# A row buffer for each half token tile in the rotation of query and key rows on GpSimd

## The chip, the cores and the metric

The kernel runs on one core of one Trainium2 chip. The metric is the device time of one execution in microseconds (us), as the median of several. Five engines work side by side and each has its own instruction queue: TensorE (PE; its weight loads are listed as PEld), VectorE (DVE), ScalarE (ACT), GpSimd (POOL) and SyncE (SP). Order between engines is kept by semaphores alone: one instruction increments a counter, another waits for it to reach a value. Transfers between HBM (the memory outside the core) and SBUF (the memory in it) run on 16 DMA engines. They are issued from the queue of SP, ACT or POOL, and each increments its semaphore by 16 once its data has landed.

## The reference

The kernel computes one layer of an encoder for 1280 tokens (1024 of one request group and 256 of another) of width 1024. Cut to what matters here:

```python
h = rmsnorm(x, norm_mix)
proj = h @ w_in                     # GLA q/k/v/gate, decay codes, GQA q/k/v, two branch gates
o_a = gla_branch(...)               # gated linear attention, forward and backward scans
o_b = gqa_branch(aq, ak, av, ...)   # 8 query heads, 2 key heads of 128
merged = sigmoid(z_a) * (o_a @ w_o_gla) + sigmoid(z_b) * (o_b @ w_o_att)
x = x + merged @ w_out
x = x + expert_choice_ffn(rmsnorm(x, norm_ffn))   # 16 experts

# within gqa_branch: the part that GpSimd prepares
qh = apply_rope(rmsnorm(qh, q_norm), cos, sin) * HD ** -0.5
kh = apply_rope(rmsnorm(kh, k_norm), cos, sin)

def apply_rope(x, cos, sin):        # pairs of neighbouring elements
    x0, x1 = x[..., 0::2], x[..., 1::2]
    return interleave(x0 * cos - x1 * sin, x0 * sin + x1 * cos)
```

## The kernel before

The program is a row of phases: `project`, `gla`, `mix`, `keys`, `attention`, `mix`, `finish_mixer`, `choose`, `experts`. Each phase is a block with a program for every engine. At its end all engines meet at a barrier (the engines report to a semaphore called gather, on which GpSimd waits, and wait themselves for one called release); a small block on GpSimd clears the phase's semaphores (`Phase.clear`, L95 to L103); then the engines meet again and jump to the next phase. Nothing of a phase starts before the last engine has left the one before.

The change lies in `project`. Tokens are in ten tiles of 128 (NT = 10). After the norm and the transposes of the token tiles, the 5,000-odd columns of `w_in` that this phase needs are taken in units of 512: seven units (NB) with the tokens in the partitions, stored in `proj_t`; two (NA) with the channels in the partitions, stored in `proj_c`; at last the 48 columns of the decay codes, which stay in SBUF. For each unit ACT issues the load of its 2 MB of weights, rounds them to a high part (`hi`, L297), DVE subtracts to get the low part (`lo`, L355), PE multiplies in three passes (L108 to L110 and L121), ACT copies each finished bank to a stage (L302) and SP stores it (L191). The last work of ACT in the phase is the copy of the decay codes (L332).

The first three units hold the attention's queries (1024 columns), keys (256) and values (256). Once their stores have landed (`stored`, 3 x 10 tiles), GpSimd turns the ten heads of each token tile, five heads (HH) at a time, which is half a token tile: 128 partitions x 640 columns, 320 KB. That is `rotate(n, h)`, L224 to L261, for n = 0 to 9 and h = 0, 1:

- it issues the read of the half from `proj_t` into `gamma` (L230), a tile that held the norm's gains earlier; for h = 0 also the reads of the tile's cosines and sines (L233); then it waits for what it issued (L235, L236);
- it squares (L237), sums over each head in seven halving adds (L240), copies the five sums into `ss` (L243), multiplies with the norm's gains into `scaled` (L247), and writes the two outputs of the rotation back over the row (L253 to L256, twice);
- it issues the write of the row back to `proj_t` (L259) and waits until it has landed (L260).

There is one row buffer and one semaphore each for reads and writes. `ph.settle` is an increment of a semaphore that nobody waits for. Of GpSimd's results nothing is used before the `keys` phase, two phases later.

Of the kernel before, what the change touches and what calls it, by code (L numbers as in the profile page):

```python
# [16 lines left out]
P = 128  # L17
# [3 lines left out]
NT, NTS = T // P, TS // P  # L21
# [5 lines left out]
AH, KVH, HD = 8, 2, 128  # L27
# [19 lines left out]
CR = 8  # L47
# [79 lines left out]
def pairs(t, e):  # L127

    return t.rearrange("... (d e) -> ... d e", e=2)[..., e]


def project(nc, x, w_cols, norm_mix, qk_norms, cos, sin, cst, act_hl, proj_t, proj_c, codes, ss):
# [3 lines left out]
    with ExitStack() as ctx:  # L136
        ph = Phase(nc, ctx, "pj")
        RC = 3 * RANK
        gamma = ph.sb("gamma", [P, D])
# [15 lines left out]
        stored = ph.stored("stored", 2)  # L155

        HH = HEADS // 2
        heads = gamma[:, 0:HH * HD].rearrange("p (h d) -> p h d", d=HD)
        scaled, first, second = ph.sb("h_scaled", [P, HH, HD]), ph.sb("h_first", [P, HH, HD // 2]), ph.sb("h_second", [P, HH, HD // 2])
        tab, gains = ph.sb("tables", [P, 2, HD // 2]), ph.sb("qk_gains", [P, 2, HD])  # L160
        gains_in, tab_in, h_in, h_back = (ph.landed(n) for n in ("gains_in", "tab_in", "h_in", "h_back"))
        h_step = ph.done("h_step")
        WIDTHS = [HD >> i for i in range(1, HD.bit_length())]
        HSTEPS = 10 + len(WIDTHS)
        x_d = x.rearrange("(n p) d -> p n d", p=P)
        w_d = w_cols.rearrange("(k p) c -> p k c", p=P)
        t_d = proj_t.rearrange("(n p) c -> p n c", p=P)
# [17 lines left out]
        with nc.Block() as block:  # L185

            @block.sync
            def _(sp):
                def store(q, s, dst, width):
                    sp.wait_ge(p_out, CR + q + 1)  # L190
                    sp.dma_start(dst, stage[:, s, 0:width]).then_inc(stored[s], 16)  # L191

                ph.start(sp)

                def load_x(n, s, i):

                    sp.wait_ge(x_ready, CR + n - 1)
                    sp.dma_start(xt[:, s], x_d[:, bass.ds(n, 1)].rearrange("p n d -> p (n d)")).then_inc(x_in[s], 16)

                tiles(sp, load_x, lambda: sp.dma_start(raw[:, 0], w_d[:, :, 0:UW]).then_inc(w_in[0], 16))  # L200
                sp.wait_ge(h_lo, CR + NT)
                sp.dma_start(raw[:, 1], w_d[:, :, UW:2 * UW]).then_inc(w_in[1], 16)
                with sp.Fori(0, NB) as n:
                    for t in range(NT):
                        store(n * NT + t, t % 2, t_d[:, t, bass.ds(n * UW, UW)], UW)
                with sp.Fori(0, NA) as n:
                    for q in range(3 * MU):
                        a, b = TOK3[q % 3]
                        store(tok_n + n * (3 * MU) + q, q % 2, proj_c[bass.ds(n * UW + q // 3 * P, P), a:b], b - a)
                for s in range(2):  # L210
                    sp.wait_ge(stored[s], ST + 16 * (tok_n + chan_n) // 2)

            @block.gpsimd
            def _(pool):
                pool.dma_start(gamma[:], norm_mix.to_broadcast([P, D])).then_inc(gamma_in, 16)
                pool.dma_start(rraw[:], w_d[:, :, (NA + NB) * UW:(NA + NB) * UW + RC]).then_inc(r_in, 16)
                pool.wait_ge(h_lo, CR + NT)
                for j, g in enumerate(qk_norms):
                    pool.dma_start(gains[:, j], g.to_broadcast([P, HD])).then_inc(gains_in, 16)
                pool.wait_ge(gains_in, 32)  # L220
                for s in range(2):
                    pool.wait_ge(stored[s], ST + 16 * G_V * NT // 2)

                def rotate(n, h):  # L224

                    c = 2 * n + h
                    b = CR + HSTEPS * c
                    rows = t_d[:, bass.ds(n, 1), h * HH * HD:(h + 1) * HH * HD].rearrange("p n c -> p (n c)")
                    flat = gamma[:, 0:HH * HD]
                    pool.dma_start(flat, rows).then_inc(h_in, 16)  # L230
                    if h == 0:
                        for j, src in enumerate((cos, sin)):
                            pool.dma_start(tab[:, j], src.rearrange("(n p) d -> p n d", p=P)[:, bass.ds(n, 1)].rearrange("p n d -> p (n d)")  # L233
                                           ).then_inc(tab_in, 16)
                        pool.wait_ge(tab_in, 32 * n + 32)  # L235
                    pool.wait_ge(h_in, 16 * c + 16)  # L236
                    pool.tensor_tensor(scaled[:], heads, heads, ALU.mult).then_inc(h_step, 1)  # L237
                    pool.wait_ge(h_step, b + 1)
                    for i, w in enumerate(WIDTHS):
                        pool.tensor_tensor(scaled[:, :, 0:w], scaled[:, :, 0:w], scaled[:, :, w:2 * w], ALU.add).then_inc(h_step, 1)  # L240
                        pool.wait_ge(h_step, b + 2 + i)
                    ph.settle(pool)
                    pool.tensor_copy(ss[:, bass.ds(n, 1), h * HH:(h + 1) * HH].rearrange("p n h -> p (n h)"), scaled[:, :, 0]).then_inc(h_step, 1)  # L243
                    b = b + len(WIDTHS)
                    pool.wait_ge(h_step, b + 2)
                    for sl, g in ((slice(0, 3), 0), (slice(3, HH), h)):
                        pool.tensor_tensor(scaled[:, sl], heads[:, sl],  # L247
                                           gains[:, g:g + 1].broadcast_to([P, sl.stop - sl.start, HD]), ALU.mult).then_inc(h_step, 1)
                    pool.wait_ge(h_step, b + 4)
                    cs, sn = (tab[:, j:j + 1].broadcast_to([P, HH, HD // 2]) for j in range(2))  # L250
                    for e, op in ((0, ALU.subtract), (1, ALU.add)):

                        pool.tensor_tensor(first[:], pairs(scaled[:], e), cs, ALU.mult).then_inc(h_step, 1)  # L253
                        pool.tensor_tensor(second[:], pairs(scaled[:], 1 - e), sn, ALU.mult).then_inc(h_step, 1)
                        pool.wait_ge(h_step, b + 6 + 3 * e)
                        pool.tensor_tensor(pairs(heads, e), first[:], second[:], op).then_inc(h_step, 1)  # L256
                        pool.wait_ge(h_step, b + 7 + 3 * e)
                    ph.settle(pool)
                    pool.dma_start(rows, flat).then_inc(h_back, 16)  # L259
                    pool.wait_ge(h_back, 16 * c + 16)  # L260
                    ph.settle(pool)  # L261

                with pool.Fori(0, NT) as n:
                    for h in range(2):
                        rotate(n, h)

            @block.scalar
            def _(act):
# [1637 lines left out]
def program(nc, dram):  # L1906

    with ExitStack() as ctx:
# [26 lines left out]
        with ExitStack() as mixer:  # L1935
            act_hl = mixer.enter_context(nc.sbuf_tensor("act_hl", [P, 2, KC, T], F32R))
            ss = mixer.enter_context(nc.sbuf_tensor("head_squares", [P, NT, HEADS], F32))
            with ExitStack() as scan:
                codes = scan.enter_context(nc.sbuf_tensor("codes", [3 * RANK, T], F32))
                project(nc, dram["x"], dram["w_cols"], dram["norm_mix"], (dram["q_norm"], dram["k_norm"]), dram["cos"], dram["sin"],  # L1940
                        cst, act_hl, proj_t, proj_c, codes, ss)
                gla(nc, proj_t, proj_c, z_c, o_t, dram["w_z"], (dram["w_gk_f"], dram["w_gk_b"]), (dram["b_gk_f"], dram["b_gk_b"]),
                    dram["gla_norm"], dram["masks"], codes, cst, act_hl)
            mix(nc, "mg", act_hl, dram["w_o_gla"], z_c[0:D], gla_g, source=o_t)
            with ExitStack() as kvs:
                kT = kvs.enter_context(nc.sbuf_tensor("kT", [P, 2, KVH, T], F32R))
                vv = kvs.enter_context(nc.sbuf_tensor("vv", [P, 2, NT, KVH * HD], F32R))
                inv = kvs.enter_context(nc.sbuf_tensor("head_inverses", [P, NT, HEADS], F32))
                keys(nc, proj_t, ss, inv, cst, kT, vv)
                attention(nc, proj_t, inv, cst, kT, vv, act_hl)  # L1950
            mix(nc, "ma", act_hl, dram["w_o_att"], z_c[D:2 * D], merged, add=gla_g)
# [55 lines left out]
```

## Time and profile before

| | before |
|---|---|
| median of 3 runs | 3467.0 us (3466.13 to 3467.72) |
| the profiled execution, whole | 3462.08 us |
| its span, first to last instruction | 3460.5 us |
| PE busy in the span | 3064.7 us (89%) |
| DVE busy | 1703.2 us (49%) |
| ACT busy | 1516.4 us (44%) |
| POOL busy | 555.5 us (16%) |
| mean granted clock of TensorE | 0.94 |

The numbers of the profile come from one execution, which here was 4.9 us shorter than the median of the three timed runs. Times in rows are microseconds from the start of the span, durations in ns or us as the view says. The page draws the span in 40 slices of 86.5 us. "Idle before" is time in which an engine stood still just ahead of an instruction, and the name behind the arrow is what ended it; "issue" there means that the profile shows nothing that it waited for.

### The profile page before, as it was taken

Reading aid. Unit: us, or ns where it says so; the run is one execution under the profiler, and the core shown is the slowest. Engines: PE = TensorE matmul, PEld = TensorE weight load, DVE = VectorE, ACT = ScalarE, POOL = GpSimd, SP = SyncE. Lnnn points to the kernel's source line nnn. Section 1 sums busy time; section 2 is a strip of 40 time slices with the busy share of each in tenths; the row PEclk is TensorE's granted clock in tenths of the full one; section 3 lists DMA queues with packets and bytes.
Section 4 is the critical chain, followed back from the end, with each engine's and each line's share of the span. In section 5 each row is a group of like instructions: output and inputs, shape, how many; then the busy total and the mean of one; then the engine's idle time right before and its main releaser. Section 6 shows DMA issues by size and latency. Waiting matters only on the chain. (4 is left out here: it accounts for less than half of the span.)

```text
span 3460.5 us, 51737 instructions
## 1 busy us (share of the span) xinstructions
PE 3064.7 (89%) x19370; PEld 2410.2 (70%) x19370; DVE 1703.2 (49%) x1710; ACT 1516.4 (44%) x1630; POOL 555.5 (16%) x726
## 2 busy tenths in 40 slices
PE   4999996298888769997788399999999999999998
PEld 4888884176667558986667277777777777777776
DVE  4010000144434228994232666766767667666675
ACT  3111110134534216663044265656655656556554
POOL 0016666301211000000100101011111111111100
PEclk7999998599899889999999699999999999999999
DMA  4233321222222430003443478888888878888784
GB/s 153 73 106 119 112 79 60 81 83 93 73 83 68 164 110 25 18 13 113 152 150 115 157 280 285 296 291 281 297 282 284 300 278 289 291 277 284 280 284 164
DMA packets 196331, 600.82 MB, mean 174 GB/s; under 512 B 15184, under 2 KB 45536, under 8 KB 196256
## 3 DMA queue, kind: packets, MB, share of 16 engines
q1 hardware_dynamic: 167056, 509.08, 41.0%
q0 software_dynamic: 21920, 76.03, 7.5%
q10 hardware_dynamic: 7280, 14.68, 1.3%
q8 instruction: 50, 0.82, 0.1%
q14 instruction: 25, 0.20, 0.0%
HBM read 522.33 MB, written 77.33 MB: 173 GB/s over the span
## 5 line engine op out<-in xcount | busy, mean ns | idle before, releaser
L1755 DVE TENSOR_TENSOR ex_w_lo<-ex_w_raw,ex_w_hi 128x2048 fp32r<-128x2048 f32 x384 | 880.0, 2292 | 450.4 <-ACT ex_w_hi L1706 450.3
L1706 ACT ACTIVATE ex_w_hi<-ex_w_raw 128x2048 fp32r<-128x2048 f32 x384 | 735.7, 1916 | 522.0 <-PE ex_ps_s L1842 467.4
L1842 PE MATMUL ex_ps_s<-ex_w_hi,ex_xS 128*128 128x512 f32 x2048 | 578.2, 395 | 0.0
L1842 PEld LDWEIGHTS ex_ps_s<-ex_w_hi,ex_xS 128*128 128x128 f32 x2048 | 375.9, 188 | 99.4 <-issue 26.3
L1842 PE MATMUL ex_ps_s<-ex_w_lo,ex_xS 128*128 128x512 f32 x1024 | 316.4, 390 | 0.0
L1842 PE MATMUL ex_ps_s<-ex_w_hi,ex_hidS 128*128 128x512 f32 x1024 | 307.9, 403 | 0.0
L1853 PE MATMUL ex_ps_p<-ex_w_raw,ex_xP 128*32 128x256 f32 x4096 | 235.5, 382 | 0.0
L1692 POOL DMA_INDIRECT y<-ex_ye_s,ex_rows_y x16 | 43.6, 2724 | 1145.8 <-DVE ex_ye_s L1798 1145.8
L108 PE MATMUL pj_ps_tok<-pj_w_hi,act_hl 128*128 128x512 f32 x560 | 219.1, 391 | 2.7 <-DVE act_hl L350 2.7
L1842 PEld LDWEIGHTS ex_ps_s<-ex_w_lo,ex_xS 128*128 128x128 f32 x1024 | 192.2, 188 | 41.4
L109 PE MATMUL pj_ps_tok<-pj_w_lo,act_hl 128*128 128x512 f32 x560 | 218.8, 391 | 0.0
L110 PE MATMUL pj_ps_tok<-pj_w_hi,act_hl 128*128 128x512 f32 x560 | 218.8, 391 | 0.0
L355 DVE TENSOR_TENSOR pj_w_lo<-pj_w_raw,pj_w_hi 128x4096 fp32r<-128x4096 f32 x9 | 39.8, 4425 | 358.6 <-ACT pj_w_hi L297 358.6
L1842 PEld LDWEIGHTS ex_ps_s<-ex_w_hi,ex_hidS 128*128 128x128 f32 x1024 | 182.8, 188 | 46.7 <-issue 13.2
L1853 PEld LDWEIGHTS ex_ps_p<-ex_w_raw,ex_xP 128*32 128x32 f32 x4096 | 126.8, 110 | 100.3 <-issue 23.9
L302 ACT ACTIVATE pj_stage<-pj_ps_tok 128x512 f32<-128x512 f32 x70 | 41.9, 599 | 308.5 <-PE pj_ps_tok L110 308.5
L108 PE MATMUL gl_z_ps<-act_hl,gl_z_w_hi 128*128 128x512 f32 (+1 forms) x384 | 156.7, 408 | 3.9 <-ACT gl_z_stage L1035 1.9
L1842 PE MATMUL ex_ps_s<-ex_w_lo,ex_hidS 128*128 128x512 f32 x512 | 159.5, 393 | 0.0
L109 PE MATMUL gl_z_ps<-act_hl,gl_z_w_hi 128*128 128x512 f32 (+1 forms) x384 | 141.9, 370 | 0.0
L110 PE MATMUL gl_z_ps<-act_hl,gl_z_w_lo 128*128 128x512 f32 (+1 forms) x384 | 141.7, 369 | 0.0
L108 PEld LDWEIGHTS pj_ps_tok<-pj_w_hi,act_hl 128*128 128x128 f32 x560 | 105.8, 189 | 25.4 <-issue 3.1
L109 PEld LDWEIGHTS pj_ps_tok<-pj_w_lo,act_hl 128*128 128x128 f32 x560 | 105.8, 189 | 22.0
(268 smaller groups left out, 5134.3 us busy)
## 6 DMA issues: line engine op xcount, KB each, us to landing
ex_w_raw<-w_e_gate SPq DMA_DIRECT2D x128, 1024.0 KB, 11.8
ex_w_raw<-w_e_up SPq DMA_DIRECT2D x128, 1024.0 KB, 11.8
ex_w_raw<-w_e_down SPq DMA_DIRECT2D x128, 1024.0 KB, 8.7
proj_t<-pj_stage SPq DMA_DIRECT2D x70, 256.0 KB, 2.0
pj_w_raw<-w_cols ACTq DMA_DIRECT2D x7, 2048.0 KB, 8.6
gl_z_w_raw<-w_z SPq DMA_DIRECT2D x16, 512.0 KB, 3.6
gate_logits<-gl_z_stage SPq DMA_DIRECT2D x32, 256.0 KB, 2.2
pj_gamma<-proj_t POOLq DMA_DIRECT2D x20, 320.0 KB, 3.3
```

Of the source, the lines that this page charges most:

```text
L108: pe.matmul(out, a[0], b[0], start=first, stop=False)
L109: pe.matmul(out, a[0], b[1], start=False, stop=False)
L110: return pe.matmul(out, a[1], b[0], start=False, stop=last)
L302: act.activation(stage[:, s, 0:width], src, ACT.Copy).then_inc(p_out, 1)
L355: dve.tensor_tensor(wlo[:, s], raw[:, s], whi[:, s].bitcast(F32), ALU.subtract).then_inc(w_lo, 1)
L1692: pool.indirect_dma_start(dst, bass.IndirectOffsetOnAxis(ap=rows_y[j][:, 0:1], axis=0), src[:], None, compute_op=ALU.add).then_inc(scatter ...
L1706: act.activation(whl[0][:, j % NHL], raw[:, j % NRAW], ACT.Copy).then_inc(w_hi, 1)
L1755: dve.tensor_tensor(whl[1][:, j % NHL], raw[:, j % NRAW], whl[0][:, j % NHL].bitcast(F32), ALU.subtract).then_inc(w_lo, 1)
L1842: mm = pe.matmul(ps_s[:, s, c:c + 512], x(part, k), whl[w][:, j % NHL, kk, c:c + 512], start=k == 0 and part + w == 0, stop=k == 2 * PU - ...
L1853: mm = pe.matmul(ps_p[CP * c:CP * c + CP, f % 2, 0:QW], x(k, c), raw[:, j % NRAW, k % 2, QW * c:QW * c + QW], start=k == 0, stop=k == 2 * ...
```

## The change

There are now two row buffers: `row_buf[0]` is the old place in `gamma`, `row_buf[1]` a new tile `h_rows` of 128 x 640, one for each half. Reads and writes have a semaphore for each half (`h_in`, `h_back`). `rotate(n, h, follow)` no longer issues its own read. It waits for its row, does the same arithmetic, and between the multiplication with the gains and the rotation proper it calls `follow()`. For h = 0 that is `next_half`: wait until the write of the second half of the tile before has landed, issue the read of this tile's second half, and wait for the tables. For h = 1 it is `next_tile`: wait until the write of this tile's first half has landed, and issue the read of the next tile's first half. The next tile's tables are read after the second half is done. The write back is issued at the end of a half, and nothing waits for it there. The first and the last tile stand outside the loop, and the two waits for the last writes stand behind it.

```diff
-        heads = gamma[:, 0:HH * HD].rearrange("p (h d) -> p h d", d=HD)
+        row_buf = [gamma[:, 0:HH * HD], ph.sb("h_rows", [P, HH * HD])[:]]
...
-                    pool.dma_start(flat, rows).then_inc(h_in, 16)
-                    if h == 0:
-                        for j, src in enumerate((cos, sin)):
...
-                        pool.wait_ge(tab_in, 32 * n + 32)
-                    pool.wait_ge(h_in, 16 * c + 16)
+                def load_half(n, h):
+                    pool.dma_start(row_buf[h], half_rows(n, h)).then_inc(h_in[h], 16)
...
+                def rotate(n, h, follow):
+
+                    b = CR + HSTEPS * (2 * n + h)
+                    heads = row_buf[h].rearrange("p (h d) -> p h d", d=HD)
+                    pool.wait_ge(h_in[h], 16 * n + 16)
                     pool.tensor_tensor(scaled[:], heads, heads, ALU.mult).then_inc(h_step, 1)
...
+                    follow()
                     pool.wait_ge(h_step, b + 4)
...
-                    pool.dma_start(rows, flat).then_inc(h_back, 16)
-                    pool.wait_ge(h_back, 16 * c + 16)
-                    ph.settle(pool)
-
-                with pool.Fori(0, NT) as n:
-                    for h in range(2):
-                        rotate(n, h)
+                    pool.dma_start(half_rows(n, h), row_buf[h]).then_inc(h_back[h], 16)
+
+                def both(n, begin, last):
+
+                    def next_half():
+                        if not begin:
+                            pool.wait_ge(h_back[1], 16 * n)
+                            ph.settle(pool)
+                        load_half(n, 1)
+                        pool.wait_ge(tab_in, 32 * n + 32)
+                        ph.settle(pool)
+
+                    def next_tile():
+                        if not last:
+                            pool.wait_ge(h_back[0], 16 * n + 16)
+                            ph.settle(pool)
+                            load_half(n + 1, 0)
+
+                    rotate(n, 0, next_half)
+                    rotate(n, 1, next_tile)
+                    if not last:
+                        load_tables(n + 1)
+
+                load_half(0, 0)
+                load_tables(0)
+                both(0, True, False)
+                with pool.Fori(1, NT - 1) as n:
+                    both(n, False, False)
+                both(NT - 1, False, True)
+                for h in range(2):
+                    pool.wait_ge(h_back[h], 16 * NT)
```

In GpSimd's queue, inside the loop, the border between the first and the second half of a tile stood like this before (`pj_gamma` is the row buffer; DMA `proj_t<-pj_gamma` is the write back, `pj_gamma<-proj_t` the read; the names in brackets are the semaphores waited for; ISA and REGISTER_ALU are bookkeeping):

```order
L256 TENSOR_TENSOR pj_gamma<-pj_h_first,pj_h_second 128x320 [waits pj_h_step]
L257 REGISTER_ALU
L259 DMA proj_t<-pj_gamma 128x640 [waits pj_h_step]
L230 ISA [waits pj_h_back0]
L230 DMA pj_gamma<-proj_t 128x640
L236 ISA
L237 TENSOR_TENSOR pj_h_scaled<-pj_gamma 128x640 [waits pj_h_in0]
```

and stands like this now, at the same border:

```order
L260 TENSOR_TENSOR pj_gamma<-pj_h_first,pj_h_second 128x320 [waits pj_h_step]
L261 REGISTER_ALU
L263 REGISTER_ALU [waits pj_h_step]
L263 DMA proj_t<-pj_gamma 128x640
L240 TENSOR_TENSOR pj_h_scaled<-pj_h_rows 128x640 [waits pj_h_in1]
```

The wait for the write and the issue of the read have gone from between the two halves; what is left there is the wait for the read alone.

In the middle of a first half stood before, in the same queue:

```order
L247 TENSOR_TENSOR pj_h_scaled<-pj_gamma,pj_qk_gains 128x384 [waits pj_h_step]
L247 TENSOR_TENSOR pj_h_scaled<-pj_gamma,pj_qk_gains 128x256
L249 REGISTER_ALU
L253 TENSOR_TENSOR pj_h_first<-pj_h_scaled,pj_tables 128x320 [waits pj_h_step]
```

and now:

```order
L250 TENSOR_TENSOR pj_h_scaled<-pj_gamma,pj_qk_gains 128x384 [waits pj_h_step]
L250 TENSOR_TENSOR pj_h_scaled<-pj_gamma,pj_qk_gains 128x256
L228 ISA [waits pj_h_back1]
L228 DMA pj_h_rows<-proj_t 128x640
L272 ISA
L253 REGISTER_ALU [waits pj_tab_in0]
L257 TENSOR_TENSOR pj_h_first<-pj_h_scaled,pj_tables 128x320 [waits pj_h_step]
```

The read of the other half and the two waits have come in between the gains and the rotation. On the other engines the same instructions stand in the same order as before; only their line numbers differ.

## Rows read from the trace of the kernel before

**Rows 1.** The page's 40 slices: busy tenths of PE, POOL; granted clock.

```profile
PE   4999996298888769997788399999999999999998
...
POOL 0016666301211000000100101011111111111100
PEclk7999998599899889999999699999999999999999
```

**Rows 2.** The view by windows: stretch, its length, each engine's busy time (count), clock.

```profile
236.60:410.00 173.40, 173.40 (x766) 143.63 (x765) 14.57 (x4) 29.73 (x35) 109.98 (x160) 1.00 0.35 119
410.00:578.00 168.00, 164.91 (x811) 135.06 (x809) 4.43 (x1) 19.48 (x32) 102.88 (x163) 0.99 0.23 77
578.00:656.00 78.00, 0.15 (x2) 0.00 (x0) 0.00 (x0) 1.23 (x1) 48.60 (x78) 0.52 0.11 35
```

**Rows 3.** Timeline of the phase border: last work of ACT and POOL, first of `gla`.

```profile
578.19 1.23 ACT L332 ACTIVATE codes<-pj_ps_chan 48x1280 f32<-48x1280 f32 x1 [15.76 <-PE pj_ps_chan L110]
...
652.40 0.57 POOL L259 DMA_DIRECT2D proj_t<-pj_gamma  x1 [0.71 <-POOL pj_gamma L256]
661.70 1.23 DVE L1212 MEMSET gl_starts<- 128x1408 bf16 x1 [206.21 <-PEq L95]
...
668.37 9.33 PE L1238 MATMUL gl_ring<-codes,gl_w_gate 16*128 16x512 f32 x12 [90.21 <-DMA gl_bias<-b_gk_b]
```

**Rows 4.** Timeline of POOL over one token tile of the loop, from its first read.

```profile
616.16 0.55 POOL L230 DMA_DIRECT2D pj_gamma<-proj_t  x1 [2.95 <-issue]
616.75 0.53 POOL L233 DMA_DIRECT2D pj_tables<-cos  x1
617.28 0.53 POOL L233 DMA_DIRECT2D pj_tables<-sin  x1
620.27 1.24 POOL L237 TENSOR_TENSOR pj_h_scaled<-pj_gamma 128x640 f32<-128x640 f32 x1 [2.46 <-DMA pj_tables<-sin]
...
626.96 0.87 POOL L253 TENSOR_TENSOR pj_h_first<-pj_h_scaled,pj_tables 128x320 f32<-128x320 f32 x1
...
633.14 0.58 POOL L259 DMA_DIRECT2D proj_t<-pj_gamma  x1 [0.81 <-POOL pj_gamma L256]
636.35 0.55 POOL L230 DMA_DIRECT2D pj_gamma<-proj_t  x1 [2.63 <-DMA proj_t<-pj_gamma]
639.64 1.25 POOL L237 TENSOR_TENSOR pj_h_scaled<-pj_gamma 128x640 f32<-128x640 f32 x1 [2.74 <-DMA pj_gamma<-proj_t]
```

**Rows 5.** Groups of POOL's instructions by line, 236 to 656 us; idle before, its releasers.

```profile
L237 POOL TENSOR_TENSOR pj_h_scaled<-pj_gamma 128x640 f32<-128x640 f32 x20 | 24.9, 1246 | 56.1 <-DMA pj_gamma<-proj_t 28.5 <-DMA pj_tables<-sin 27.6
L230 POOL DMA_DIRECT2D pj_gamma<-proj_t x20 | 11.0, 550 | 231.3 <-DMA proj_t<-pj_stage 172.4 <-DMA proj_t<-pj_gamma 32.0 <-issue 26.9
```

**Rows 6.** Two slow transfers: the waits on the row's write, then the tables.

```profile
347.17 0.55 POOL L230 DMA_DIRECT2D pj_gamma<-proj_t  x1 [6.24 <-DMA proj_t<-pj_gamma]
...
540.61 1.24 POOL L237 TENSOR_TENSOR pj_h_scaled<-pj_gamma 128x640 f32<-128x640 f32 x1 [4.59 <-DMA pj_tables<-sin]
```

**Rows 7.** Timeline of DVE, 236 to 455 us: all its work there.

```profile
287.88 4.42 DVE L355 TENSOR_TENSOR pj_w_lo<-pj_w_raw,pj_w_hi 128x4096 fp32r<-128x4096 f32 x1 [49.98 <-ACT pj_w_hi L297]
342.27 4.42 DVE L355 TENSOR_TENSOR pj_w_lo<-pj_w_raw,pj_w_hi 128x4096 fp32r<-128x4096 f32 x1 [49.97 <-ACT pj_w_hi L297]
396.68 4.42 DVE L355 TENSOR_TENSOR pj_w_lo<-pj_w_raw,pj_w_hi 128x4096 fp32r<-128x4096 f32 x1 [49.98 <-ACT pj_w_hi L297]
451.07 4.43 DVE L355 TENSOR_TENSOR pj_w_lo<-pj_w_raw,pj_w_hi 128x4096 fp32r<-128x4096 f32 x1 [49.97 <-ACT pj_w_hi L297]
```

**Rows 8.** Timeline of POOL: the gains' multiplication, beside DVE's work and alone.

```profile
286.93 5.97 POOL L247 TENSOR_TENSOR pj_h_scaled<-pj_gamma,pj_qk_gains 128x384 f32<-128x384 f32 x2
...
310.86 1.71 POOL L247 TENSOR_TENSOR pj_h_scaled<-pj_gamma,pj_qk_gains 128x384 f32<-128x384 f32 x2
...
395.74 5.96 POOL L247 TENSOR_TENSOR pj_h_scaled<-pj_gamma,pj_qk_gains 128x384 f32<-128x384 f32 x2
```

**Rows 9.** The line L355: count, durations in ns (least/median/most).

```profile
L355 DVE TENSOR_TENSOR pj_w_lo<-pj_w_raw,pj_w_hi x9: 4424/4425/4427, 52.6 to 451.1; 128x4096 fp32r<-128x4096 f32 x9
```

**Rows 10.** Timeline at two other phase borders, into `attention` and into `choose`.

```profile
1287.74 2.83 DVE L457 TENSOR_TENSOR kT<-ky_turned,kT 128x2560 fp32r<-128x2560 f32 x1 [1.06 <-ACT kT L442]
...
1292.03 0.53 POOL L539 DMA_DIRECT2D at_q_in<-proj_t  x1 [51.33 <-SPq L83]
...
1904.45 0.27 ACT L1421 ACTIVATE affT<-fm_ps_a 16x128 f32<-16x128 f32 x1 [0.94 <-PE fm_ps_a L1499]
1905.79 0.48 DVE L1558 MEMSET tk_aff<- 96x512 f32 x1 [1.81 <-PEq L95]
```

More of the change, by code:

```diff
@@ L157, in project @@
         HH = HEADS // 2
-        heads = gamma[:, 0:HH * HD].rearrange("p (h d) -> p h d", d=HD)
+        row_buf = [gamma[:, 0:HH * HD], ph.sb("h_rows", [P, HH * HD])[:]]
         scaled, first, second = ph.sb("h_scaled", [P, HH, HD]), ph.sb("h_first", [P, HH, HD // 2]), ph.sb("h_second", [P, HH, HD // 2])
         tab, gains = ph.sb("tables", [P, 2, HD // 2]), ph.sb("qk_gains", [P, 2, HD])
-        gains_in, tab_in, h_in, h_back = (ph.landed(n) for n in ("gains_in", "tab_in", "h_in", "h_back"))
+        gains_in, tab_in, h_in, h_back = ph.landed("gains_in"), ph.landed("tab_in"), ph.landed("h_in", 2), ph.landed("h_back", 2)
         h_step = ph.done("h_step")
@@ L222, in _, with half_rows, load_tables @@
                     pool.wait_ge(stored[s], ST + 16 * G_V * NT // 2)
[L224 to L229, printed above, removed]
-                    pool.dma_start(flat, rows).then_inc(h_in, 16)
-                    if h == 0:
-                        for j, src in enumerate((cos, sin)):
-                            pool.dma_start(tab[:, j], src.rearrange("(n p) d -> p n d", p=P)[:, bass.ds(n, 1)].rearrange("p n d -> p (n d)")
-                                           ).then_inc(tab_in, 16)
-                        pool.wait_ge(tab_in, 32 * n + 32)
-                    pool.wait_ge(h_in, 16 * c + 16)
+                def half_rows(n, h):
+                    return t_d[:, bass.ds(n, 1), h * HH * HD:(h + 1) * HH * HD].rearrange("p n c -> p (n c)")
+                def load_half(n, h):
+                    pool.dma_start(row_buf[h], half_rows(n, h)).then_inc(h_in[h], 16)
+                def load_tables(n):
+                    for j, src in enumerate((cos, sin)):
+                        pool.dma_start(tab[:, j], src.rearrange("(n p) d -> p n d", p=P)[:, bass.ds(n, 1)].rearrange("p n d -> p (n d)")
+                                       ).then_inc(tab_in, 16)
+                def rotate(n, h, follow):
+                    b = CR + HSTEPS * (2 * n + h)
+                    heads = row_buf[h].rearrange("p (h d) -> p h d", d=HD)
+                    pool.wait_ge(h_in[h], 16 * n + 16)
                     pool.tensor_tensor(scaled[:], heads, heads, ALU.mult).then_inc(h_step, 1)
```

## The prediction

> **What bounds the kernel now.** I read the page's slices first. PE is at nine tenths almost everywhere except in a few holes, and one hole is the eighth slice (606 to 692 us): PE 2, clock 5, while POOL shows 3 after four slices of 6 [rows 1]. The view by windows narrows it down. From 236.6 to 578 us PE is busy for 338.3 of 341.4 us, and POOL works beside it. From 578 to 656 us PE is busy for 0.15 us, DVE for nothing, ACT for 1.23 us, and POOL alone works, for 48.60 us of 78 [rows 2]. The timeline says why: ACT's last work of the phase ends at 578.19 + 1.23 = 579.42 us, POOL issues its last write at 652.40 us, and the first work of `gla` starts on DVE at 661.70 us; PE had been idle for 90.21 us when it began again [rows 3]. All engines must have left the phase before the next one starts, so from 579.42 us on the rotation on POOL is the critical path, and nothing covers it. That is the only place where this change can gain, and it can gain no more than the gap: the end is then set by PE and ACT.
>
> Next I asked what POOL's 78 us are made of. One token tile (two halves) takes from 616.16 us to the next read, some 39.8 us. Its arithmetic is 620.27 to 633.14 us for the first half, 12.9 us with its step to the write, and about the same for the second. Between them it stands still four times: 2.46 us for the tables and the row, 2.63 us for the first write to land, 2.74 us for the second row, 2.95 us for the second write (listed as "issue", at the loop's turn) [rows 4]. Over all twenty halves the groups give 56.1 us for reads, and 32.0 + 26.9 us for writes, 115.0 us in all; the 172.4 us in the same row is the wait for the projection's first units and stays [rows 5].
>
> **The change part by part.**
>
> *The waits between halves.* A write is now waited for in the middle of the following half, a read at the start of the half after its issue. The middle of a half is 626.96 - 620.27 = 6.7 us behind its start [rows 4], the slowest write seen was waited for 6.24 us behind its issue, the slowest row or table read 4.59 us [rows 6], so each write has 6.7 us or more before somebody asks for it, and each read has the rest of its half, another 6.2 us, and the write's issue. I take both waits as gone. What stays is the first read (from 3.29 us issue to start, [rows 4]), the last write (2.6 to 2.95 us), and the turn of the loop, 0.3 us by the difference of 2.95 and 2.63, nine times. So 115.0 - 3.3 - 2.6 - 2.9 = about 106 us leave POOL's chain.
>
> *The DMA issues.* POOL still issues twenty reads, twenty writes and twenty table reads at 0.53 to 0.58 us each [rows 4]. The reads stood between halves and stand now in their middle; the count is the same and nobody but POOL waits behind them. Cost: zero, against an upper bound of 0.55 us a half, 11 us in all, if an issue in the middle holds up more than it did at the border.
>
> *Collisions with DVE.* Four times in this stretch DVE splits weights for 4.42 us [rows 7]. At 287.88 and 396.68 us POOL was in the multiplication with the gains, and the pair took 5.97 and 5.96 us in place of 1.71 us [rows 8]: 4.26 us of stall each, just under DVE's whole 4.42 us. At 342.27 and 451.07 us POOL stood in a wait for a DMA, and the stall hid there. With POOL almost never idle all four will count: two more, 8.5 us added. The Trainium skill ("GPSIMD Engine Reference", Key points) says that GpSimd shares its SBUF interfaces with VectorE and contends with DVE instructions that have two SBUF inputs. The rule speaks against this change, since denser POOL work meets more of DVE's, and the trace agrees with it; by the rule as by the rows POOL is held for at most DVE's 4 x 4.42 = 17.7 us. DVE pays nothing: its nine splits lie between 4424 and 4427 ns [rows 9], with POOL in the middle of an operation or not.
>
> *POOL's new end.* Before, POOL left at 652.40 + 0.57 + 2.6 to 2.95 = 655.6 to 655.9 us. Now 655.7 - 106 + 8.5 = 558 us; with the 11 us above, 569 us. ACT's last work ends at 579.42 us. So POOL leaves the path with 21 us to spare (10 in the worse case), and the phase ends with ACT. From there on a faster POOL is worth nothing: of the 98 us that it gains, some 21 are lost as slack.
>
> *PE's stretch.* It stays: PE was busy for 173.40 of 173.40 us while POOL worked for 109.98 us beside it [rows 2], and its order is unchanged.
>
> *The barrier.* This is the one term that the trace does not show directly. Before, from POOL's leaving (655.7) to the first work of `gla` (661.70, [rows 3]) it took 6.0 us. At two borders where another engine than POOL came last it took 1905.79 - 1904.72 = 1.07 us (behind ACT, as here in future) and 1292.03 - 1290.57 = 1.46 us (behind DVE) [rows 10]. So `gla` begins between 580.5 and 585.4 us. I take the nearest kind of border, one with ACT last, near the short end: 580.9 us, since POOL will have come out of its loop long before. The extra 4.6 us I can't explain from the rows; they may belong to POOL's exit from the loop or to this border as such.
>
> *Sum.* 661.70 - 580.9 = 80.8 us less, or 76.3 us with the long barrier. All phases behind it begin with the same barrier and the same loads and are carried forward as they are. Of TensorE: before 661 us it was granted half clock (0.52 over the gap, [rows 2]), and after some 9 us of idle I expect the same start at half clock, so no further gain. The profiled execution would take 3462.1 - 80.8 = 3381.3 us; it stood 4.9 us below the median of the runs, so the median becomes 3467.0 - 80.8 = 3386.2 us.
>
> **The rivals.**
>
> *A: the long barrier stays.* For it: the 6.0 us were measured at this very border, and the release that DVE saw last was PE's, not POOL's [rows 3]. Against: the two borders of [rows 10]. Time: 3467.0 - 76.3 = 3390.7 us.
>
> *B: POOL stays the last engine.* The mechanism: the reads are not hidden, because POOL does not go on while its own transfer is prepared and under way, and only the waits for writes fall (32.0 + 26.9 = 58.9 us, less 2.6 and 2.9 that stay: 53 us) while the two extra stalls come on top (8.5 us). POOL then leaves at 655.7 - 53 + 8.5 = 611 us, the gain is 45 us and the time 3422 us. Against: in [rows 4] the issue of a table read follows 0.04 us after the one before it, while the row's transfer is under way. In a milder form (each half some 1.1 us longer than I think) POOL ends level with ACT, and only beyond that it costs.
>
> *C: slower than before.* The mechanism: POOL's denser traffic holds up DVE's splits and with them PE. The place is the start of each unit (every 54.4 us, [rows 7]). DVE has some 50 us of idle before each split [rows 7], so each would have to grow from 4.4 to over 54 us before PE waits at all, and over the stretch PE would have to lose more than 80.8 us, a quarter of its 341 us, for the kernel to be slower. At a loss of 90 us the time would be 3476 us. Against: [rows 9], and PE's full business beside POOL [rows 2].
>
> *D: no change.* The change would have to leave the border where it is, because the end of the phase was not POOL's. The 90.21 us of PE's idle time with only POOL at work [rows 2, 3] speak against it. Time 3467 us.
>
> **How the numbers follow.** My forecast (short barrier) has 0.58, A 0.32, B in all its forms 0.07, C 0.01, D 0.01; 0.01 is left for what I haven't seen. The range must hold forecast and A with the spread of the runs (1.6 us) and a few microseconds for a `gla` that starts on another phase of the clock: 3380 to 3398 us, which leaves B and C out. A change of 0.2% is 6.9 us, about what a measurement of this kernel can tell from none. Forecast, A and B are all faster by more: 0.97; within 0.2%: 0.015; slower: 0.015.
>
> **What would show it.** Right: in the windows after, no stretch with POOL alone; the first work of `gla` at 580 to 586 us; POOL's last write issued before 570 us; idle before the squares (now L240) of 5 us or less in all instead of 56.1; a write's wait before the read in the middle of nearly nothing; four operations of POOL stretched by up to 4.4 us; the read's issue in the middle at 0.55 us; DVE's splits still 4.42 us; the last of PE's decay code matmuls ending at about 578 us. Wrong: POOL's last write behind 579 us (then B, and its idle rows say whether reads or writes), or PE ending later than 580 us (C), or `gla` beginning 6 us behind ACT (A).

## The result and the profile after

| | before | after |
|---|---|---|
| median, 4 runs each | 3467.36 us (3466.13 to 3469.76) | 3388.27 us (3381.91 to 3389.43) |
| ratio | | 0.9771, 95% interval 0.9756 to 0.9785 |
| span of the profiled execution | 3460.5 us | 3386.0 us |
| POOL busy in the span | 555.5 us | 565.6 us |

The change took 79.1 us, 2.3%. The forecast was 80.8 us less and 3386 us.

The timeline at the phase border, after, answers to [rows 3]:

```profile
546.16 0.58 POOL L263 DMA_DIRECT2D proj_t<-pj_h_rows  x1 [0.63 <-POOL pj_h_rows L260]
...
578.84 1.23 ACT L360 ACTIVATE codes<-pj_ps_chan 48x1280 f32<-48x1280 f32 x1 [15.74 <-PE pj_ps_chan L110]
581.38 1.23 DVE L1240 MEMSET gl_starts<- 128x1408 bf16 x1 [125.23 <-PEq L95]
...
588.45 9.33 PE L1266 MATMUL gl_ring<-codes,gl_w_gate 16*128 16x512 f32 x12 [9.64 <-DMA gl_bias<-b_gk_b]
```

POOL issues its last write at 546.16 us instead of 652.40 us, ACT ends the phase at 580.07 us, and `gla` begins 1.31 us later. PE stands still for 9.64 us where it stood still for 90.21 us. The start of `gla` moved by 661.70 - 581.38 = 80.3 us.

The view by windows, after, answers to [rows 2] (the last column pair is DMA share and GB/s):

```profile
237.00:410.00 173.00, 173.00 (x765) 143.23 (x764) 15.04 (x4) 29.64 (x35) 150.53 (x220) 1.00 0.38 132
410.00:540.00 130.00, 130.00 (x640) 109.58 (x639) 4.42 (x1) 16.63 (x27) 113.21 (x174) 1.00 0.27 92
```

POOL is now busy for 87% of its stretch, and PE for all of it, as before.

The groups of POOL's instructions, after, answer to [rows 5] (busy us, mean ns, then idle before):

```profile
L240 POOL TENSOR_TENSOR pj_h_scaled<-pj_h_rows 128x640 f32<-128x640 f32 x10 | 12.7, 1266 | 0.2
L240 POOL TENSOR_TENSOR pj_h_scaled<-pj_gamma 128x640 f32<-128x640 f32 x10 | 12.6, 1264 | 2.6 <-DMA pj_gamma<-proj_t 2.4
...
L228 POOL DMA_DIRECT2D pj_h_rows<-proj_t x10 | 5.7, 570 | 0.0
L228 POOL DMA_DIRECT2D pj_gamma<-proj_t x10 | 5.7, 567 | 172.4 <-DMA proj_t<-pj_stage 172.4
```

Of 56.1 us of read waits 2.8 are left, of 58.9 us of write waits none; the 172.4 us are the start of the stretch. The wait for the very last write is in neither sum, since no read stands behind it. A read's issue in the middle of a half takes 0.57 us, the same as at the border.

The span shrank by 74.5 us, 5.8 less than the border moved. In the profiled execution after, `gla` took 474.9 us against 471.9, and the stretch from `attention`'s first read to the phase behind it 296.9 us against 294.9. Over the thirteen traces of this study, twelve have an unchanged `gla` and it took 469.2 to 475.8 us in them; all thirteen have an unchanged `attention` and it took 294.4 to 297.6 us. So this is a spread that comes without any edit there.

### The profile page after: what moved, and what is told of

The parts are those of the page before. It is cut to its first block and busy times, and to the rows that moved or that the text cites. A ratio compares the mean times of both kernels' runs of the same rounds, so it can differ in the third digit from the quotient of the medians.

```text
span 3386.0 us, 51643 instructions
## 1 busy us (share of the span) xinstructions
PE 3069.7 (91%) x19370; PEld 2413.4 (71%) x19370; DVE 1703.3 (50%) x1710; ACT 1516.0 (45%) x1630; POOL 565.6 (17%) x726
## 5 line engine op out<-in xcount | busy, mean ns | idle before, releaser
L1870 PEld LDWEIGHTS ex_ps_s<-ex_w_hi,ex_hidS 128*128 128x128 f32 x1024 | 182.8, 188 | 46.8 <-issue 13.2
L108 PEld LDWEIGHTS pj_ps_tok<-pj_w_hi,act_hl 128*128 128x128 f32 x560 | 105.8, 189 | 25.4 <-issue 3.0
L110 PEld LDWEIGHTS pj_ps_tok<-pj_w_hi,act_hl 128*128 128x128 f32 x560 | 105.7, 189 | 22.2
```

What stands on the lines that cost most here:

```text
L108: pe.matmul(out, a[0], b[0], start=first, stop=False)
L110: return pe.matmul(out, a[1], b[0], start=False, stop=last)
L1870: mm = pe.matmul(ps_s[:, s, c:c + 512], x(part, k), whl[w][:, j % NHL, kk, c:c + 512], start=k == 0 and part + w == 0, stop=k == 2 * PU - ...
```

## The experiments

All but e8 and e9 are read at the start of `gla` (DVE's memset of `gl_starts`), which the spread of the later phases does not reach: the changed kernel, the same kernel again (e11) and e3 have it at 581.38, 580.92 and 580.55 us. A ratio is that to the kernel before in the same set of runs, which is why medians of different experiments are not compared to the microsecond.

### Half of the change at a time

e1 keeps the read ahead and waits for each write at once:

```diff
                     pool.dma_start(half_rows(n, h), row_buf[h]).then_inc(h_back[h], 16)
+                    pool.wait_ge(h_back[h], 16 * n + 16)
+                    ph.settle(pool)
...
-                        if not begin:
-                            pool.wait_ge(h_back[1], 16 * n)
-                            ph.settle(pool)
```

(and the same wait in `next_tile`). 

> One half of the change: two row buffers and the read of the next half issued in the middle of this one, but each write back is waited for at once, as before. Theory (the phase ends with the later of POOL and ACT, and the waits between halves add up): the 56.1 us of read waits go but for the first 3, the 58.9 us of write waits stay, one or two more collisions with the weight splits on DVE are added (4 to 9 us). POOL issues its last write at about 604 to 608 us and stays the last engine; gla begins at 609 to 617 us; the kernel takes about 3417 to 3424 us against 3388 for the whole change. Rival (one of the two waits alone was the obstacle, since read and write share one queue and one hides behind the other): the last write is issued before 580 us or still after 640 us.

e2 waits for writes late and reads at the start of each half:

```diff
+                    for h in range(2):
+                        if not begin:
+                            pool.wait_ge(h_back[h], 16 * n)
+                            ph.settle(pool)
+                        load_half(n, h)
...
+                        rotate(n, h)
```

> The other half of the change: two row buffers, each write back waited for only when its buffer is to be read into again, but each read issued at the start of its own half and waited for at once. Theory: the 58.9 us of write waits go but for the last 3, the 56.1 us of read waits stay, 4 to 9 us of collisions are added. POOL issues its last write at about 601 to 606 us, gla begins at 606 to 615 us, the kernel takes about 3413 to 3422 us. Rival (a read issued right behind a write on the same queue must wait for that write to be moved): the read waits grow from 2.7 us each by up to 2.5 us, and POOL gains almost nothing: last write after 640 us, over 3450 us.

| | last write issued | `gla` begins | median | ratio to before |
|---|---|---|---|---|
| before | 652.40 | 661.70 | | |
| e1 | 588.00 | 597.42 | 3401.51 | 0.9824 (0.9808 to 0.9841) |
| e2 | 595.22 | 604.56 | 3411.45 | 0.9851 (0.9832 to 0.9869) |
| after | 546.16 | 581.38 | 3388.27 | 0.9771 (0.9756 to 0.9785) |

Both halves leave POOL last, and each alone gives most of the gain (64.3 and 57.1 of 80.3 us at the start of `gla`): as far as the mechanism goes the theory holds and the rivals fall. But both missed their expected ranges: the last write came 6 to 20 us earlier than expected, and the median of e1 is 15 us below its range. The groups of e1, then of e2, say why:

```profile
L250 POOL TENSOR_TENSOR pj_h_scaled<-pj_gamma,pj_qk_gains 128x384 f32<-128x384 f32 (+1 forms) x20 | 17.1, 878 | 0.8
L240 POOL TENSOR_TENSOR pj_h_scaled<-pj_h_rows 128x640 f32<-128x640 f32 x10 | 12.5, 1250 | 28.8 <-DMA proj_t<-pj_gamma 28.8
...
L232 POOL DMA_DIRECT2D pj_tables<-cos x10 | 5.4, 537 | 29.4 <-DMA proj_t<-pj_h_rows 29.4
```

```profile
L240 POOL TENSOR_TENSOR pj_h_scaled<-pj_h_rows 128x640 f32<-128x640 f32 x10 | 12.5, 1250 | 34.2 <-DMA pj_h_rows<-proj_t 34.2
L240 POOL TENSOR_TENSOR pj_h_scaled<-pj_gamma 128x640 f32<-128x640 f32 x10 | 12.5, 1250 | 28.7 <-DMA pj_tables<-sin 28.7
```

e1 keeps 58.2 us of write waits and e2 62.9 us of read waits, near the 58.9 and 56.1 us of the sums. What was wrong was the sign of the collisions. I had added 4 to 9 us for them; in e1 it was 0.7 us (the squares' group, 13.2 us in place of 12.5) and in e2 nothing, because DVE's splits fell into waits and issues of transfers, so the 8.5 us that the kernel before paid went away. Where a stall falls is chance as long as there are waits.

That the 58.2 us come so near the 58.9 is partly chance too. The timeline of e1 at the second and the fourth split (342.26 and 451.06 us):

```profile
338.43 0.38 ACTq L317 DMA_DIRECT2D pj_w_raw<-w_cols  x1
...
347.51 0.54 POOL L232 DMA_DIRECT2D pj_tables<-cos  x1 [6.14 <-DMA proj_t<-pj_h_rows]
...
453.67 0.54 POOL L232 DMA_DIRECT2D pj_tables<-cos  x1 [2.66 <-DMA proj_t<-pj_h_rows]
...
454.75 1.84 POOL L240 TENSOR_TENSOR pj_h_scaled<-pj_gamma 128x640 f32<-128x640 f32 x1
```

Some 4 us before each of the first three splits ACT issues the load of the next 2 MB of weights, which lands 9.3 to 9.7 us later; from 340 to 347.5 us the 16 DMA engines are busy all the time. The three writes of e1 that fell beside it were waited for 5.57, 6.14 and 5.21 us in place of 2.08 or 2.66, which is 10 us of the 58.2; the kernel before has one such wait (6.24 us). At the fourth split there are no more weights to load: the wait is the usual 2.66 us, and the rest of the split is paid by the squares (1.84 us in place of 1.25). So the split by itself does not lengthen a transfer; the load is the likely cause, though no row has a load without a split right behind it. In e2 two of the ten reads of second rows fell there (4.67 and 4.61 us); the eight others took 3.1 us against 2.85 before, and only that difference can come from the order, a read right behind a write.

e1 less its collisions gained 64.4 - 7.8 = 56.6 us, e2 57.2 - 8.5 = 48.7 us, together 105.3; the whole change, 106.2 us with 7.4 us more of stalls, is 113.6 without them. The 8 us between lie within what e2 keeps: 6.8 us of longer read waits and 4.8 us of short pauses ahead of its reads.

### POOL's slack

e3, e7 and e4 put 16, 24 and 48 operations that nobody uses behind the last half of the changed kernel:

```diff
+                for i in range(48):
+                    pool.tensor_tensor(scaled[:], scaled[:], scaled[:], ALU.subtract).then_inc(h_step, 1)
+                    pool.wait_ge(h_step, at + i + 1)
                 for h in range(2):
                     pool.wait_ge(h_back[h], 16 * NT)
```

> The changed kernel with 16 idle-work operations of 128x640 on POOL behind the last half, about 1.33 us each, 21 us in all. Theory (POOL has 31 us of slack behind its last write): POOL finishes at about 570 us, ACT at 580 us, gla begins at 581.4 us as without the pad, and the time is that of the changed kernel, 3388 us within 3. Rival (the end of the phase hangs on POOL in some way that the trace does not show, such as its release from the barrier): up to 21 us more, 3409 us.

> The changed kernel with 48 such operations in straight line behind the last half, 64 us in all, so that POOL is the last engine again, at about 611 us, but leaves without a loop and without a transfer to wait for. Theory on slack: the phase ends 31 us later than in the changed kernel, so 64 - 31 + a border = 3388 + 31 = about 3419 us. On the border there are two theories: the 6.0 us of the kernel before belonged to POOL's leaving a loop as the last engine: then gla begins 1.1 to 1.6 us behind the last operation here; or they belong to POOL being last at all: then 5 to 6 us.

e5 has the 48 in a loop, `with pool.Fori(0, 48) as i:`, around the same two lines. 

> As the kernel with 48 idle operations in straight line, but the 48 stand in a loop of one operation, which POOL leaves as the last engine. If the long border of the kernel before (6.0 us) comes from leaving a loop last, gla begins 5 to 6 us behind the last operation here and 1.1 to 1.6 us in the straight-line version. If it comes from POOL being last at all, both show 5 to 6 us. If it comes from the wait for a write back right before the border, both show the short border.

e6 is the kernel before with its last token tile out of the loop:

```diff
-                with pool.Fori(0, NT) as n:
+                with pool.Fori(0, NT - 1) as n:
                     for h in range(2):
                         rotate(n, h)
+                for h in range(2):
+                    rotate(NT - 1, h)
```

> The kernel before with its last token tile taken out of the loop, nothing else. POOL still ends the phase at about 655.5 us behind a wait for a write, but in straight-line code. If the long border comes from the exit of the loop: gla begins 1.1 to 2 us behind 655.5 us in place of 6.0 us, and the kernel is about 4.5 us faster than before, 3462.5 us (the exit of the loop one tile earlier may cost the same 4.6 us there, which then eats the gain: last write at 657 us, gla at 658 to 662 us, and no difference). If it comes from POOL being last or from waiting for a write: gla begins 6 us behind POOL and the time is 3467 us.

> The changed kernel with 24 idle operations in straight line on POOL, 32 us in all, so that POOL's last operation ends at about 578.3 us, 2 us before ACT's at about 580. Theory (GpSimd needs some 5.4 us more than the other engines between its last operation and its arrival at the barrier, measured as 6.8 and 7.0 us from its last operation to gla against 1.3 behind ACT): POOL arrives at 583.7 us and gla begins at about 585 us, 3.5 us later than in the changed kernel. Rival (the long border comes only when POOL is the last to finish its work): ACT ends last here, and gla begins 1.3 us behind ACT, at 581.4 us.

| | POOL's last operation ends | ACT's ends | `gla` begins | median |
|---|---|---|---|---|
| e3 | 567.76 | 579.25 | 580.55, 1.30 behind ACT | 3385.73 |
| e7 | 579.38 | 579.63 | 586.14, 6.76 behind POOL | 3387.14 |
| e4 | 610.47 | 579.96 | 617.23, 6.76 behind POOL | 3420.68 |
| e5 | 623.57 | 579.40 | 630.54, 6.97 behind POOL | 3432.52 |
| e6 | 652.18 (write issued) | 579.73 | 660.76, 8.58 behind it | 3463.17 |

For e6 the second column has the end of the last write's issue, and the median of e5 is of two runs. e3: 21 us of added work on POOL cost nothing. e4: 64 us cost 35.9 us at the border. So the phase ends with the later of two arrivals, as the theory had it. The border itself is longer in e4 and e5 than the 5 to 6 us expected at most. The timeline of e7 says whose it is:

```profile
547.45 31.93 POOL L294 TENSOR_TENSOR pj_h_scaled<-pj_h_scaled 128x640 f32<-128x640 f32 x24
...
578.40 1.23 ACT L364 ACTIVATE codes<-pj_ps_chan 48x1280 f32<-48x1280 f32 x1 [15.74 <-PE pj_ps_chan L110]
586.14 1.23 DVE L1244 MEMSET gl_starts<- 128x1408 bf16 x1 [130.43 <-PEq L95]
```

ACT finishes last here, by 0.25 us, and the border is long all the same. The rival (long only if POOL finishes last) falls: POOL needs 5.5 us more than ACT from its last operation to the barrier (6.76 against 1.30). Its slack in the changed kernel is therefore not 31 us but about 25. It isn't the loop either: straight line and loop show 6.76 and 6.97 us, and e6, whose write lands about 2.5 us after its issue, some 6 us, as before. The ratio of e6 to before is 0.9994 (0.9985 to 1.0004), no difference. Nor is it a wait for a write: in e4 the last one had landed some 60 us before.

The view by source line names it. Line 185 is the block of the phase, and at its end every engine has a DRAIN in its queue, which the timelines leave out. ACT and POOL in the kernel before, then POOL in e7 (durations in ns, then the start):

```profile
L185 ACTq DRAIN  x1: 1259/1259/1259, 578.2 to 578.2; - x1
L185 POOLq DRAIN  x1: 5293/5293/5293, 655.1 to 655.1; - x1
```

```profile
L185 POOLq DRAIN  x1: 5289/5289/5289, 579.6 to 579.6; - x1
```

ACT's runs beside its last activation and ends with it, at 579.45 us. POOL's begins when all its work and waits are done and takes 5.29 us, in every one of the thirteen traces. Before, it ends at 655.1 + 5.3 = 660.4 us and `gla` begins 1.3 us later; in e7 it ends at 584.9 us and `gla` begins 1.3 us later, as it does behind ACT. In the changed kernel it runs from 549.2 to 554.5 us and nobody waits for it.

### Is it GpSimd's exit in general?

e8 adds eight such operations on POOL at the end of `gla`, where POOL issues no transfers; e9 a memset and eight of 128x640 at the end of the first `mix`, where it does. Each makes POOL the last engine in that phase:

```diff
+                for i in range(8):
+                    pool.tensor_tensor(kt[:, 1], kt[:, 1], kt[:, 1], ALU.subtract).then_inc(k1_prod, 1)
+                    pool.wait_ge(k1_prod, CR + GH + i + 1)
```

and in e9, with a new tile `idle` and a semaphore `idled`:

```diff
+                    pool.wait_ge(gated, CR + NT8)
+                    pool.memset(idle[:], 1.0).then_inc(idled, 1)
...
+                    for i in range(8):
+                        pool.tensor_tensor(idle[:], idle[:], idle[:], ALU.subtract).then_inc(idled, 1)
+                        pool.wait_ge(idled, CR + i + 2)
```

> The changed kernel with eight idle operations of 128x1280 (2.9 us each) on POOL at the end of the gla phase, in which POOL issues no transfer, so that POOL is the last engine there, about 20 us behind SP's last store. If the long border is GpSimd's in general, the next phase's first transfer comes 6.5 to 7 us behind POOL's last operation. If it belongs to the projection phase, or to a phase in which POOL issues transfers, it comes 1.3 to 2 us behind.

> The changed kernel with nine idle operations on POOL (128x640, about 11 us in all) at the end of the first mix phase, behind its last gated product, so that POOL is the last engine there. In that phase POOL issues transfers, as in the projection. If the extra 5.5 us at a border belong to a phase in which POOL issues transfers, the first work of the keys phase (ACT's) comes about 6.8 us behind POOL's last operation. If they belong to the projection's border alone, it comes 1.3 to 2 us behind, as it did behind gla.

The timelines of e8, then of e9:

```profile
1048.77 19.09 POOL L1018 TENSOR_TENSOR gl_k_t<-gl_k_t 128x1280 f32<-128x1280 f32 x8
1069.41 0.95 POOL L778 DMA_DIRECT2D mg_w_raw<-w_o_gla  x1 [1.55 <-SPq L83]
```

```profile
1189.82 10.56 POOL L791 TENSOR_TENSOR mg_idle<-mg_idle 128x640 f32<-128x640 f32 x8
1202.29 1.28 ACT L464 ACT_TABLE_LOAD   x1 [33.10 <-PEq L95]
1202.75 0.95 SPq L459 DMA_DIRECT2D ky_kv<-proj_t  x2
```

1.55 us (POOL's own first transfer) and 1.91 us (ACT's table load) behind POOL's last operation: both borders are short, and POOL's DRAIN takes 0.04 us in e8 and 1.04 us in e9. So the long border is not GpSimd's in general. But e9 does not clear phases in which it issues transfers. In the kernel before, where no work stands behind the last transfer, the DRAIN at the end of the two `mix` phases (line 731) is the longest that POOL has:

```profile
L731 POOLq DRAIN  x2: 7260/7543/7826, 1240.2 to 1686.7; - x2
```

The first ends at 1247.4 us, 24 us before the next phase begins, so it costs nothing there. In `mix` the nine added operations went with a DRAIN of 1.0 us; in the projection 48 of them left it at 5.29 us. What sets its length stays open.

### What bounds the phase now

In the changed kernel PE waits 3.1 us for the last group of banks before the decay codes, although they use the other group's. e10 waits for that one only:

```diff
-                pe.wait_ge(p_out, CR + tok_n + chan_n)
+                pe.wait_ge(p_out, CR + tok_n + chan_n - 3)
```

> The changed kernel with one number changed on PE: before the matmuls of the decay codes it waits until the last but one group of banks is copied out, whose banks they use, and not for the last group too. Theory (with POOL off the path the projection phase ends with PE and ACT, so what PE saves there is saved in the kernel): PE's idle 3.09 us ahead of the first of these matmuls goes, and with it the half clock of the first ones (0.43 us apart instead of 0.23, about ten of them, 2 us). ACT's copy of the codes ends at about 575 us and gla begins at 576.3 us, 5 us earlier than in the changed kernel, 3383 us. Rival (the end is still POOL's, whose arrival is at about 554 us by its last transfer): no change in the start of gla.

> The changed kernel once more, on the same chip as the version with the early decay codes, as its control: 3388 us within 3, gla begins at 581.4 us within 1.

The timelines of e10, then of e11:

```profile
573.26 1.23 ACT L360 ACTIVATE codes<-pj_ps_chan 48x1280 f32<-48x1280 f32 x1 [9.44 <-PE pj_ps_chan L110]
575.80 1.23 DVE L1240 MEMSET gl_starts<- 128x1408 bf16 x1 [120.44 <-PEq L95]
```

```profile
562.82 0.40 PE L108 MATMUL pj_ps_chan<-act_hl,pj_r_hi 128*48 128x512 f32 x1 [3.10 <-ACT pj_stage L330]
...
578.38 1.23 ACT L360 ACTIVATE codes<-pj_ps_chan 48x1280 f32<-48x1280 f32 x1 [15.71 <-PE pj_ps_chan L110]
580.92 1.23 DVE L1240 MEMSET gl_starts<- 128x1408 bf16 x1 [124.83 <-PEq L95]
```

`gla` begins 5.1 us earlier, as expected, and both parts of the saving are there: PE doesn't wait for the last group of banks, and its clock doesn't fall (granted clock 1.00 from 560 to 568 us, where the changed kernel had 0.67 and 0.65 behind its wait). The median of e11 is 3.4 us below the 3388 expected, 0.4 us outside its range, and its border is inside. The medians are 3378.99 us (five runs, 3377.67 to 3386.71) and 3384.59 us (3382.52 to 3387.68); against the kernel before the ratios are 0.9764 (0.9750 to 0.9778) and 0.9773 (0.9759 to 0.9787). The intervals overlap, so by the whole time e10 is only likely to be the fastest of all; by the border it is earlier, and it confirms that PE and ACT set the phase's end.

## Why the prediction was right

**The bound.** Right. POOL alone held the phase for 76 us, and the gain stopped where ACT ends. The sum over POOL's waits would have given 106 us; 79.1 came.

**The waits between halves.** Right. 112.2 of 115.0 us of idle time went; I had 106 us. Two terms that I took off were wrong: the turn of the loop (2.9 us) was hidden like the rest, and the wait for the last write (2.6 us) had never been in the 115.0, which are waits ahead of reads. The write waits of the slow kind vanished too, as their cover of 6.7 us said.

**The DMA issues.** Right, nearly zero: 0.57 us in the middle against 0.55, 0.4 us for all twenty.

**The collisions.** The count was right, and their full cost nearly. All four of DVE's splits held POOL up, by 3.8 to 4.1 us; for example, after:

```profile
288.94 4.07 POOL L246 COPY head_squares<-pj_h_scaled 128x5 f32 x1 [0.25 <-POOL pj_h_scaled L243]
...
451.93 4.97 POOL L257 TENSOR_TENSOR pj_h_first<-pj_h_scaled,pj_tables 128x320 f32<-128x320 f32 x1
```

The copy takes 0.19 us and the product 0.89 us elsewhere. DVE's share was not quite nothing: three of its four splits took 4.44 to 4.55 us in place of 4.42, 0.24 us in all (up to 4.79 us in e11), and nobody waited for them. The bound of 17.7 us held, with 15.9 us measured; it was worked out from the rows alone.

**POOL's new end.** Mis-sized on the safe side: forecast 558 us, measured 546.16 + 0.58 and some 2.5 us until the write lands, 549 us. Of the 9 us, some 6 are waits that I had left in (112.2 against 106) and 1.1 the stalls (7.4 us added, not 8.5); the last 2 us I can't assign.

**The barrier.** Right in size, 1.31 us for a forecast of 1.1 to 1.5, but without its reason. I had two guesses for the other 4.6 us, POOL's exit from its loop or this border as such. e5 and e6 rule out the loop; e7 and the view of line 185 show that the cost is POOL's DRAIN of 5.29 us between its last operation and the barrier, so that it is hidden when POOL is done 5.5 us before the others. The trace of the kernel before had that row already. That the short border came was right by the analogy with other borders, not by knowing the cause. Rival A named the right border, but with POOL early it had no way to act.

**PE's stretch.** Right: ACT's last work moved from 579.42 to 580.07 us, and of those 0.65 us all were there before POOL's first read (DVE's split began at 234.12 us in place of 233.47).

**The rest.** `gla` began at half clock again (0.50 granted from 581.3 to 588.4 us), as forecast. "All phases behind it are carried forward as they are" holds in the median, not for one trace against another: there 5.8 us were lost in phases whose spread is as large.

## What to carry to other kernels

When one engine works alone before a barrier, price a change to it by the gap to the next engine's last work, not by the waits that it removes: here 106 us left POOL's chain and 79 us the kernel. A read issued half a step ahead, with the write waited for half a step later, hides both transfers as long as half a step (6.7 us here) is longer than the longest wait for a transfer (6.2 us); it cost no more issues, but 7.4 us more of stalls beside VectorE, here off the critical path. A pause before a barrier is looked up by the source line of the block, since the timelines leave out a DRAIN. And compare two traces at a fixed border, since single executions differ by more than a small edit.

## What the runs showed of the hardware

A 4.42 us subtraction on VectorE from two SBUF tiles stopped what GpSimd computed beside it for nearly its whole length, down to a copy of five elements a row (0.19 us became 4.07). A wait of GpSimd for a transfer was not lengthened by it (2.66 us at the fourth split of e1, as elsewhere). That made the stall's cost depend on where GpSimd stood: 15.9 us in the changed kernel, 8.5 before, 0.7 in e1, none in e2. The Trainium skill ("GPSIMD Engine Reference", Key points) names DVE instructions with two SBUF inputs as contending with GpSimd; these rows agree.

Beside a 2 MB load of another queue a write of 320 KB took 5.6 to 6.1 us from issue to landing, against 2.5 us without it, so what GpSimd saves in stalls by waiting there it pays in part as a longer wait.

And before the barrier at a phase's end GpSimd has a DRAIN, which the timelines leave out: 5.29 us in the projection whatever stood ahead of it, 7.3 and 7.8 us in the two `mix` phases of the kernel before, 0.04 and 1.04 us where e8 and e9 put plain operations ahead of it.
